# Cross attention of a transformer trunk: output in token pairs, two split slabs held, hidden rows turned in two PSUM places, scores inside the next query product

## What is computed

```python
def cross_attn(h, m, wq, wkv, wo):
    q = (h @ wq).reshape(B, S, CROSS_HEADS, CROSS_HEAD_DIM)
    kv = (m @ wkv).reshape(B, m.shape[1], 2, CROSS_HEADS, CROSS_HEAD_DIM)
    k, v = kv[:, :, 0], kv[:, :, 1]
    s = jnp.einsum('bthd,bmhd->bhtm', q, k) * CROSS_HEAD_DIM ** -0.5
    p = jax.nn.softmax(s.astype(jnp.float32), axis=-1).astype(v.dtype)
    return jnp.einsum('bhtm,bmhd->bthd', p, v).reshape(B, S, D_MODEL) @ wo
...
        x = x + rmsnorm(merged @ w_out[l], g[NORM_POST_MIX])
        h = rmsnorm(x, g[NORM_PRE_CROSS])
        m = rmsnorm(mem, g[NORM_MEM])
        x = x + rmsnorm(cross_attn(h, m, cross_wq[l], cross_wkv[l], cross_wo[l]), g[NORM_POST_CROSS])
        h = rmsnorm(x, g[NORM_PRE_MLP])
        x = x + rmsnorm(jnp.square(jax.nn.relu(h @ mlp_w1[l])) @ mlp_w2[l], g[NORM_POST_MLP])
```

## Time and profile before

| | before |
|---|---|
| time, median of 3 runs | 1527.98 us (1526.26 to 1528.58) |
| the profiled execution's own time | 1525.69 us |
| span of the profile | 1523.9 us |
| mean granted clock of TensorE | 0.996 of full speed |
| TensorE busy | 1469.6 us (96%) |
| VectorE, ScalarE, GpSimd busy | 680.6, 570.4, 121.9 us |
| DMA moved | 137.87 MB, mean 90 GB/s |

### The profile page before, as it was taken

One profiled execution on the slowest core, in us unless ns is written; L12 is line 12 of the kernel. 1 busy time (PEld: TensorE's weight loads), 2 busy tenths in 40 slices (PEclk: granted clock), 3 DMA queues, 4 the chain that ended last, 5 costly groups with the idle time before them and its releaser, 6 DMA issues.

```text
span 1523.9 us, 17320 instructions
## 1 busy us (share of the span) xinstructions
PE 1469.6 (96%) x7180; PEld 1183.3 (78%) x7180; DVE 680.6 (45%) x1170; ACT 570.4 (37%) x920; POOL 121.9 (8%) x90
## 2 busy tenths in 40 slices
PE   6999999999999999999999999899989999999997
PEld 5957778887887788876776788786668888888886
DVE  3656566755343454464355235652236323122334
ACT  4445542214333334345345315443334332223321
POOL 1000000022220000000000110001210110001100
PEclk9999999999999999999999999999999999999999
DMA  5211132232322244441110433261122323232221
GB/s 175 80 35 45 48 105 83 84 110 69 97 66 73 64 138 158 146 125 38 33 55 29 152 111 111 84 215 62 55 72 67 93 101 104 90 94 100 104 90 55
DMA packets 118270, 137.87 MB, mean 90 GB/s; under 512 B 7043, under 2 KB 98432, under 8 KB 118192
## 3 DMA queue, kind: packets, MB, share of 16 engines
q1 hardware_dynamic: 115200, 126.17, 25.8%
q0 software_dynamic: 2704, 10.00, 1.9%
q10 hardware_dynamic: 288, 0.59, 0.1%
HBM read 134.61 MB, written 2.14 MB: 90 GB/s over the span
## 4 chain that ended last, share of the span: by engine, by line
PE 90%; DVE 4%; ACT 4%; issue 1%; DMA 0%; SPq 0%; DVEq 0%; ACTq 0%
PE dense L627 24%; PE dense L629 24%; PE dense L628 24%; PE score L740 3%; PE turned L757 3%; PE score L757 3%; PE turned L740 2%; PE turned L750 1%; PE score L730 1%; PE score L750 1%; DVE probs L1806 1%; ACT probsT L1210 1%; ACT weight_high L1210 1%; PE score L1143 1%; PE turned L1123 1%
## 5 line engine op out<-in xcount | busy, mean ns | idle before, releaser
L1652 DVE TENSOR_TENSOR weight_low<-raw,weight_high 128x2048 fp32r<-128x2048 f32 (+2 forms) x98 | 205.8, 2106 | 377.7 <-ACT weight_high L1210 377.7
L627 PE MATMUL dense<-hidden_high,weight_high 128*128 128x512 f32 (+1 forms) x840 | 324.3, 386 | 3.1 <-ACT vN L1210 2.5
L1210 ACT ACTIVATE weight_high<-raw 128x2048 fp32r<-128x2048 f32 (+4 forms) x158 | 224.6, 1446 | 267.6 <-PE dense L629 265.1
L629 PE MATMUL dense<-hidden_high,weight_low 128*128 128x512 f32 (+1 forms) x840 | 320.9, 382 | 0.0
L628 PE MATMUL dense<-hidden_low,weight_high 128*128 128x512 f32 (+1 forms) x840 | 320.5, 382 | 0.0
L627 PEld LDWEIGHTS dense<-hidden_high,weight_high 128*128 128x128 f32 x840 | 158.5, 189 | 33.0 <-ACT vN L1210 2.9
L629 PEld LDWEIGHTS dense<-hidden_high,weight_low 128*128 128x128 f32 x840 | 158.3, 188 | 30.9
L628 PEld LDWEIGHTS dense<-hidden_low,weight_high 128*128 128x128 f32 x840 | 158.5, 189 | 29.5 <-issue 0.2
L1647 DVE TENSOR_TENSOR weight_low<-raw,weight_high 128x1024 fp32r<-128x1024 f32 x58 | 74.9, 1334 | 73.6 <-ACT weight_high L1210 73.6
L627 PE MATMUL dense<-weight_high,up_high 128*128 128x512 f32 x256 | 99.7, 389 | 1.7 <-DVE weight_low L1652 1.7
L629 PE MATMUL dense<-weight_high,up_low 128*128 128x512 f32 x256 | 99.6, 389 | 0.0
(11 more groups left out here) (299 smaller groups left out, 2344.9 us busy)
## 6 DMA issues: line engine op xcount, KB each, us to landing
raw<-in_w_in SPq DMA_DIRECT2D x34, 1024.0 KB, 5.3
raw<-in_mlp_w SPq DMA_DIRECT2D x32, 1024.0 KB, 5.1
raw<-in_w_branch SPq DMA_DIRECT2D x12, 1024.0 KB, 5.2
raw<-in_nsa_cmp_w SPq DMA_DIRECT2D x8, 1024.0 KB, 5.5
raw<-in_cross_wkv SPq DMA_DIRECT2D x8, 1024.0 KB, 5.5
raw<-in_w_in SPq DMA_DIRECT2D x9, 512.0 KB, 5.1
bias_strips<-bias_scratch POOLq DMA_DIRECT2D x8, 512.0 KB, 4.1
raw<-in_w_out SPq DMA_DIRECT2D x4, 1024.0 KB, 4.9
```

Source lines behind the costliest of these rows:

```text
L627: pe.matmul(out_ap, ah, bh, start=first, stop=False)
L629: return pe.matmul(out_ap, al, bh, start=False, stop=last)
L1210: return nc.scalar.activation(dst, src, ACT.Copy, scale=scale)
L1652: ins = V.tensor_tensor(dst, src, hi.bitcast(F32), ALU.subtract)
```

## The change

1. **Hidden rows.** `score0` and `score1` become the halves of one PSUM tensor `SS`. Turned rows go to `W` for even tiles and `SS` for odd ones. `turn_hidden_rows(0, 0)` stands behind key product 3, the turns 1 to 3 behind the first three value slabs. The queues of ScalarE and VectorE follow: the row chain of `wo` is spread between the splits of the key slabs.
2. **Scores.** The four score tiles of head n - 1 stand inside query product n, ahead of chunks 1 to 4 of its eight, and the two groups of turned probabilities ahead of chunks 6 and 7. `cross_values(n - 1)` keeps its place behind the product. Head 3's scores run alone; its turns and values stand between the first output tiles. The normalising multiply of the probabilities moves from GpSimd to VectorE.
3. **Cross output.** Slab order (0, 0), (1, 0), (0, 1), (1, 1). Token tiles 0 and 1 run through all four slabs first, then tiles 2 and 3. The first and the last slab keep their split parts in places of their own (`heldH`, `heldL`: 16 KB each over memory and later over keys and values that are no longer read), so that they can serve both pairs. Half n of the width has its own `G`. Turns of rows 0 and 1 stand behind the first and second n = 0 slab of pair 1; row 2 behind `up_half(0, 0)`, row 3 ahead of chunk 6 of `up_half(1, 0)`.
4. **Last down product.** Tiles 0 and 1 use slab 2, then both slab 3, then tiles 2 and 3 as before.

The core of the diff:

```diff
...
+        heldH = [at("held_high0", [P, KD, SW], 96, F32R), at("held_high1", [P, KD, SW], 112, F32R)]
+        heldL = [at("held_low0", [P, KD, SW], 104, F32R), at("held_low1", [P, KD, SW], 120, F32R)]
...
-        S = [ps("score0", [P, T]), ps("score1", [P, T])]
+        SS = ps("score", [P, 2, T])
+        S = [SS[:, 0, :], SS[:, 1, :]]
...
-        for n in range(2):
-            for kk in range(2):
+        for kk in range(2):
+            for n in range(2):
                 row_slab(("co", n, kk), rows("cross_wo"), n, kk)
...
+        place_free = {s: used_at[s - 2] for s in range(2, SLABS)}
+        place_free[slab_at["co", 0, 0]] = ready_at["cv", 1]
+        place_free[slab_at["co", 0, 1]] = used_at[slab_at["cq", 2]]
+        place_free[slab_at["co", 1, 1]] = ready_at["cq", 3]
+        place_free[slab_at["up", 0, 1]] = used_at[slab_at["co", 1, 0]]
...
             def turn_hidden_rows(j, t):
 
                 pe.wait_ge(hrow_ready[j], t + 1)
-                if t:
-                    pe.wait_ge(hlow[j], t)
+                if t >= 2:
+                    pe.wait_ge(hlow[j], t - 1)
                 for k in range(KD):
-                    mm = pe.transpose(W[:, k // 4, k % 4 * P:(k % 4 + 1) * P], yN[:, t, k * P:(k + 1) * P], ident[:, :])
+                    mm = pe.transpose((W, SS)[t % 2][:, k // 4, k % 4 * P:(k % 4 + 1) * P], yN[:, t, k * P:(k + 1) * P], ident[:, :])
                 mm.then_inc(hturned[j], 1)
...
-                turn_hidden_rows(0, n)
+                if n == GROUPS - 1:
+                    turn_hidden_rows(0, 0)
...
+                    if 2 * n + kk < NT - 1:
+                        turn_hidden_rows(0, 2 * n + kk + 1)
...
+            def cross_score(n, i):
+
+                if i == 0:
+                    pe.wait_ge(taken["A"], taken_count[product_at["cq", n]])
+                m = n * NT + i
+                if m >= 2:
+                    pe.wait_ge(cross_taken, m - 1)
+                if n and i == 1:
+                    pe.wait_ge(catt_taken, 2 * n)
+                for b in range(2):
+                    mm = pe.matmul(S[m % 2][:, 0:MEM], qT[:, b, i * P:(i + 1) * P], kxT[:, 2 * n + b, :], start=b == 0, stop=b == 1)
+                mm.then_inc(cross_ready, 1)
+
+            def query_chunk(n):
+
+                def at_chunk(k):
+                    if n and 1 <= k <= NT:
+                        cross_score(n - 1, k - 1)
+                    if n and k >= KD - 2:
+                        cross_turn(n - 1, k - KD + 2)
+                return at_chunk
...
-                t_mode(slab_at["cq", n], two(g), both, KD, hT).then_inc(product_ready, 1)
+                t_mode(slab_at["cq", n], two(g), both, KD, hT, query_chunk(n)).then_inc(product_ready, 1)
                 if n:
                     cross_values(n - 1)
...
+            for i in range(NT):
+                cross_score(GROUPS - 1, i)
...
+            co_tile(0, 0, 0)
+            cross_turn(3, 0)
+            co_tile(0, 0, 1)
+            cross_turn(3, 1)
+            co_tile(1, 0, 0)
+            cross_values(3)
+            co_tile(1, 0, 1)
+            for n in range(2):
+                for t in range(2):
+                    co_tile(n, 1, t)
+            for n, kk in ((0, 0), (0, 1), (1, 0), (1, 1)):
+                for t in range(2, NT):
+                    co_tile(n, kk, t)
+                if n == 0:
+                    turn_hidden_rows(1, kk)
...
             up_half(0, 0)
-            turn_hidden_rows(1, 3)
-            free_rows(("co",), 1)
-            up_half(1, 0)
+            turn_hidden_rows(1, 2)
+            up_half(1, 0, lambda k: turn_hidden_rows(1, 3) if k == KD - 2 else None)
...
-                        for t in range(NT):
-                            for kk in range(2, 4):
-                                mm = rows_tile(slab_at["down", f, n, kk], name, t, up, 4 * kk, False, kk == 3)
-                                if kk == 3 or t == NT - 1:
-                                    mm.then_inc(product_ready, 1)
+                        for t, kk in ((0, 2), (1, 2), (0, 3), (1, 3), (2, 2), (2, 3), (3, 2), (3, 3)):
+                            mm = rows_tile(slab_at["down", f, n, kk], name, n, t, up, 4 * kk, False, kk == 3)
+                            if kk == 3 or t == NT - 1:
+                                mm.then_inc(product_ready, 1)
...
-            for t in range(NT):
-                pre_root(0, t)
-            for n in range(GROUPS):
-                high(slab_at["ck", n] + 2)
-                hidden_tile_high(0, n)
+            high(slab_at["ck", 0] + 2)
+            pre_root(0, 0)
+            high(slab_at["ck", 1] + 2)
+            pre_root(0, 1)
+            pre_root(0, 2)
+            high(slab_at["ck", 2] + 2)
+            pre_root(0, 3)
+            high(slab_at["ck", 3] + 2)
+            hidden_tile_high(0, 0)
...
             for n in range(GROUPS):
+                row_residual(0, n)
+                if n == 3:
+                    hidden_row(0, 1)
+                    hidden_row(0, 2)
                 cross_key(n)
-                hidden_tile_low(0, n)
-                if n == 0:
-                    hidden_row(0, 3)
+                if n == 1:
+                    hidden_row(0, 0)
+            hidden_row(0, 3)
+            hidden_tile_low(0, 0)
...
-                V.reciprocal(rtotal[:, 0:4], total[:, 0:4]).then_inc(crt_ready, 1)
+                link(V.reciprocal(rtotal[:, 0:4], total[:, 0:4]))
+                for i in range(NT):
+                    ins = V.tensor_scalar(probX[:, i, :], probX[:, i, :], rtotal[:, i:i + 1], None, ALU.mult)
+                ins.then_inc(cprobs_ready, 1)
...
+            row_evict(1, ("co",), 1, 2)
+            row_sum(1, 2)
+            row_residual(1, 2)
+            low(slab_at["co", 1, 1] + 2)
+            row_evict(1, ("co",), 1, 3)
+            row_sum(1, 3)
+            hidden_row(1, 2)
+            row_residual(1, 3)
+            hidden_row(1, 3)
+            for t in range(2, NT):
+                hidden_tile_low(1, t)
```

More of the change, by code:

```diff
@@ L439, in row_products @@
             for t in range(NT):
[L440 removed]
+                if t == 0:
                     part(slab_at[(*name, 1, 0)])
@@ L451, in layer @@
             product(("cq", n), "A", slab_at["cq", n])
-        row_products(("co",))
+        for pair in range(2):
+            for kk, n in ((0, 0), (0, 1), (1, 0), (1, 1)) if pair == 0 else ((0, 0), (1, 0), (0, 1), (1, 1)):
+                if kk == 0:
+                    part(slab_at["co", n, 0])
+                else:
+                    for t in (2 * pair, 2 * pair + 1):
+                        product(("co", n, t), "V", slab_at["co", n, 1])
         for f in range(2):
@@ L1029, in free_tile, with rows_tile @@
                 pe.wait_ge(taken[takers[g]], taken_count[g])
-            def rows_tile(s, name, t, act, a0, first, last):
-                high, low = wide(wh[s % 2], 4, T), wide(wl[s % 2], 4, T)
+            def rows_tile(s, name, n, t, act, a0, first, last):
+                high, low = wide(split_high(s), 4, T), wide(split_low(s), 4, T)
                 c = slice(t * P, (t + 1) * P)
@@ L1039, in rows_tile @@
                         slab_half(s, 1)
-                    mm = blocks3(tile_bank(name, t), (act[0][:, a0 + k, c], act[1][:, a0 + k, c]), (high[:, k, :], low[:, k, :]),
+                    if name == ("co",) and t < 2:
+                        pe.wait_ge(catt_taken, a0 + k + 1)
+                    mm = blocks3(row_bank(name, n, t), (act[0][:, a0 + k, c], act[1][:, a0 + k, c]), (high[:, k, :], low[:, k, :]),
                                  first and k == 0, last and k == 3)
@@ L1157, in up_half @@
+            def up_half(n, half, at_chunk=None):
                 c = slice(half * 2 * P, (half + 1) * 2 * P)
@@ L1557, in cross_turned, with cross_exps @@
                     copy(coH[:, 2 * n + b, :], (OT, S[1])[b][:, :]).then_inc(catt_high, 1)
-            for n in range(GROUPS):
-                ready(("cq", n))
-                copy(qT[:, :, :], bank(("cq", n))[:, :, :], CROSS_SCALE).then_inc(taken["A"], 1)
-                if n:
-                    cross_turned(n - 1)
+            def cross_exps(n):
                 for i in range(NT):
@@ L2078, in cross_low, with cross_probs @@
                     V.tensor_tensor(coL[:, c, :], (OT, S[1])[b][:, :], coH[:, c, :].bitcast(F32), ALU.subtract).then_inc(catt_taken, 1)
-            for n in range(GROUPS):
-                if n:
-                    cross_low(n - 1)
+            def cross_probs(n):
                 for i in range(NT):
```

234 lines of the change are left out of this document (123 added, 111 removed).

## The result

The changed kernel takes 1501.88 us (median of 4 runs, 1501.19 to 1502.69), the kernel before 1527.12 (4 runs, 1525.93 to 1528.58). The ratio is 0.9833, 95% interval 0.9821 to 0.9845: 25.2 us or 1.7% faster. The prediction was 1507.9 with a range of 1502 to 1515.

The account below looks back on a forecast made before the run. TensorE, busy 96% of the span, was taken as the bound, so time could be won only from its waits, restarts and lower clock. Gains 7.3 + 4.6 + 6.5 + 1.7 = 20.1 us gave 1505.6, plus 2.3 to the median: 1507.9, range 1502 to 1515.

Parts of the forecast that it names:

- the second low-clock stretch: Cross output, around 1163.5 to 1166.9 us: clock near 0.5 after a 2.0 us wait, said to cost more than the wait.
- Part 2: Query products: scores inside the next product, rounds of 19.55 instead of about 21.05 us, gain 4.6 us.
- Part 1: Memory keys and values: hidden rows turned later, in two places, 56.2 to 48.9 us, gain 7.3 us.
- The late maxima of the first round: First query round: VectorE splits query slab 2 first, so maxima start 2 us late, costing 0.5 us.
- Part 3: Cross output to third up product: token pairs with two slabs held, 83.41 to 76.9 us, gain 6.5 us.
- The sure wait: Second up half, up_half(1, 0): TensorE waits 1.1 us for the last hidden low part.
- The wait of 0.5 for row tile 2: Output stage: TensorE waits 0.5 us because that tile's hidden_row stands behind the split of up slab 1.
- Part 4: Last down product: new order puts 2.7 us more work ahead of a 1.7 us slab wait, gain 1.7 us.
- Rival 2: Whole change: nothing waits and restarts hide, gain 26 us, so 1502 us; chance 0.10.
- Queues as new waits: Rival: VectorE and ScalarE queues become the new wait, gain 12 us, so 1516 us; chance 0.15.
- Lower clock in the rounds: Rival: granted clock falls in the query rounds and output stage, up to 1562 us; chance 0.04.
- That nothing is gained: Rival: another wait stands behind each removed one, 1525 to 1531 us; chance 0.03.

Follow-up runs that it names:

- experiment 1: The kernel before, unchanged, timed and profiled a second time: ratio 1.0001 to the kernel before.
- Experiment 8: The changed kernel with the first turn of hidden rows moved up, behind key product 1 instead of 3: 1509.87 us, ratio 0.9882 to the kernel before.
- Experiment 9: The changed kernel with all turned hidden rows in the one place W again: 1508.69 us, ratio 0.9879 to the kernel before.
- experiment 6: The changed kernel with score tiles two by two, ahead of chunks 1 and 4: 1500.95 us, ratio 0.9826 to the kernel before.
- experiment 7: The changed kernel with the normalising multiplies back on GpSimd: 1517.05 us, ratio 0.9931 to the kernel before.
- experiment 4: The changed kernel with the old tile-by-tile order of the last down product: 1503.60 us, ratio 0.9847 to the kernel before.
- experiment 5: The changed kernel, unchanged, timed and profiled a second time: 1502.02 us, ratio 0.983 to the kernel before.
- experiment 2: The kernel before with only the hidden rows turned later and in two PSUM places: 1519.15 us, ratio 0.9944 to the kernel before.

## Why the prediction came out as it did

**What failed.** The mechanism held: nearly every wait that was forecast to go went, each part paid in its own stage, and all four gains were forecast too small. Two sizes were wrong. The term of Part 2, a score tile at 1.00 us and a round at 19.55, measured 0.93 on average and 18.99; with the smaller misses of the other parts the sum was 3.4 us short. And the base: 2.3 us were added for the distance between a profiled execution and the median, which the changed kernel did not show.

**What bounds the kernel.** Right: the gain came out of TensorE's waits, restarts and low clock. Wrong in one point: the second low-clock stretch cost nothing (experiment 1), because the chain of the next row set the end of the stage.

**Part 1**, 7.3 forecast, 7.8 measured. The queue bookkeeping held: value slab 0, which I had 0.8 us ahead of its need, made no wait, and the first query product started at 1019.35 (forecast 1019). The 0.5 too little is mostly double counting: the 5.84 us of a key product had been read behind a turn, with a restart in it, and another restart was added behind each turn; the four in a row took 23.03 us, not 23.4. Experiment 8 shows what stood behind it: the wait and the clock together. Experiment 9 shows that the second place is part of the gain: the wait it saves is 3.4 us.

**Part 2**, 4.6 forecast, 6.3 measured. This is the term that was mis-sized. I priced a tile inside a product at the 0.78 to the next start plus 0.22 that the product behind it ran long. The 0.22 holds; the 0.78 came from a tile that had waited, and a tile that has not takes 0.67. Inside a product a tile cost 0.89, 0.92, 0.99 and 0.92, 3.72 for four, not 4.0; the 0.99 is the one that waits a little (experiment 6), so my sentence that these waits all go was not quite right. The values with their restart took 3.45, not 3.64, and the wait of 0.1 for the multiplies was none. That is 0.6 a round. The late maxima of the first round did cost 0.4 of the 0.5 that I had, 0.3 of it wait; the first two products with their scores took 29.87, 10.88 + 18.99, only because no values stand ahead of that round and their restart of 0.4 falls away. That this came out even is luck. It comes back at the end: the values of head 2 with the scores of head 3 behind them took 0.4 more than values ahead of a product, and those scores 4.67 instead of 4.60, together the 0.5 that I had too little there. The move of the multiplies was right in mechanism and in size (1.14 us, 0.16 us to spare), and it is what the part needs: experiment 7.

**Part 3**, 6.5 forecast, 7.5 measured. The sure wait came, 0.95 us of the 1.1 forecast, for the reason given; timeline of all engines in the changed kernel, the turn, its two copies and the product:

```profile
1153.17 1.04 PE L1081 MATMUL score<-ident,y_rows 128*128 128x128 f32 x8
1154.24 1.02 ACT L1268 ACTIVATE hidden_high<-score 128x1024 fp32r<-128x1024 f32 x1 [2.82 <-PE score L1081]
1155.30 1.23 DVE L2124 TENSOR_TENSOR hidden_low<-score,hidden_high 128x1024 fp32r<-128x1024 f32 x1 [2.14 <-ACT hidden_high L1268]
...
1156.58 0.39 PE L660 MATMUL dense<-hidden_high,weight_high 128*128 128x256 f32 x1 [0.95 <-DVE hidden_low L2124]
```

The wait of 0.5 for row tile 2 did not come: its row was ready at 1147.54, 0.45 us ahead of the turn, so my chain was some 0.9 us too long. I had added up whole durations, while instructions in one queue overlap by some 0.08 us at their ends (four multiplies of 0.35 took 1.14); over five or six hand-overs that is half of it, and the rest was not traced. The other 0.5 is small change: no wait of 0.1 for the multiplies, 0.15 of the sure wait, and some 0.2 in all for up halves that had a restart counted twice, as in Part 1, and for values.

**Part 4**, 1.7 forecast, 2.0 measured: the wait, and the restart behind it, which I had not counted. In experiment 4 the two matmuls around the wait start 2.06 us apart, 1.83 more than the pace of 0.23 (the waits view counts only from the end of a record), and the next is another 0.11 late.

**The range.** Terms too small by 3.4 us, and a base: I added 2.3 us for the distance of the median of before from its profiled execution, as if the same distance held for the changed kernel, whose profile lay 0.8 above its median. In experiment 5 the same kernel's profile lay 1.5 below it, so the distance depends on which execution was profiled. With exact terms the sum would have been 1504.5; the 2.6 us between that and the result are this base, the largest single miss (0.9 of it because the median of before came out at 1527.12 in the result and not at 1527.98). Either miss alone would have left the time inside the range, at 1504.5 or 1505.3. Rival 2 (nothing waits, restarts hide) at 1502 was nearest; it went too far on the restarts and not far enough on the base. Its bound stood as the edge of the range, with nothing left below it.

**The other rivals.** Queues as new waits: no, the only new wait is the 0.95. Lower clock in the rounds: the windows show 1.00 in the changed kernel with six changes of kind in each round. With a wait of 2.3 us added to each round (experiment 7) the clock did fall behind the first and the third, and not behind the second. The Trainium skill, TensorE: Matmul & The Clock Gate, section "A second HAM failure mode: psum-queue depth-cycling", tells of short idle times between groups of matmuls that made the clock swing. In this trace the changes of kind, with waits of at most 0.3 us, did not bring it about. That nothing is gained: no.

## What to carry to other kernels

When one engine is busy 96% of the time, cut the span into stages, hold each against the undisturbed pace of that engine, and place the other queues by durations: here the sum came out within 0.3 to 1.7 us for each stage. Take the price of a tile or a turn from one that has not waited, take the pace of a product from one with nothing ahead of it, and count each restart once. Small work is best put inside a big product where its chain through the other engines is shorter than the chunks behind it, and the engine of each link in that chain must be chosen by that count: 1.14 or 3.6 us for the same four multiplies decided some 15 us. And test a wait at its place before blaming it: removing one may only show the next chain behind it. The distance between one profiled execution and a median belongs to that execution, and is not to be carried over to another kernel.

## What was unexpected of the hardware

A wait of 2.0 us in the same place of the same kernel was followed by a granted clock near 0.5 in two of three profiles and by 1.00 in the third, and the stage took 83.41 us each time. In experiment 2 it was the 2.2 us wait ahead of it that a fall followed, which it did in no profile of before, and the stage took 84.80. The other stages without an edit repeat within 0.1 us between executions, while the first 970 us vary by 3.0 us.
